# First projection block: the high part of x runs ahead of its low part, and the filter network's second layer moves four steps later

## The reference, cut to what matters

```python
xn = _rmsnorm(x, attn_norm_w)
proj = xn @ w_in                      # 1952 columns: hyena streams, q and kv latents, rotary key

h = jnp.sin(freq * (z @ filt_w1 + filt_b1))
h = jnp.sin(freq * (h @ filt_w2 + filt_b2))
h = h @ filt_w3                       # the implicit filters, multiplied by a decay table
```

## Time and profile before

| | |
|---|---|
| median of three runs | 1778.93 us (1777.25 to 1779.46) |
| the profiled execution, its own time | 1777.29 us |
| its span, first to last instruction | 1775.5 us |
| TensorE matmuls busy | 1730.4 us, 97% of the span, 10563 matmuls |
| DVE / ACT / POOL busy | 75% / 41% / 23% |
| mean granted TensorE clock | 0.996 |

### The profile page before, as it was taken

One profiled execution on the slowest core, in us unless ns is written; L12 is line 12 of the kernel. 1 busy time (PEld: TensorE's weight loads), 2 busy tenths in 40 slices (PEclk: granted clock), 3 DMA queues, 4 the chain that ended last, 5 costly groups with the idle time before them and its releaser, 6 DMA issues.

```text
span 1775.5 us, 26444 instructions
## 1 busy us (share of the span) xinstructions
PE 1730.4 (97%) x10563; PEld 1581.4 (89%) x10563; DVE 1338.2 (75%) x1677; ACT 728.8 (41%) x1149; POOL 407.8 (23%) x256
## 2 busy tenths in 40 slices
PE   7999999999999999998999999999899999999999
PEld 5776888887999988887999999999899999998887
DVE  6894676978998986779655555558999898996634
ACT  6122321166787785245333333334333333334411
POOL 0000000002222220003121222115758373740000
PEclk9999999999999999999999999999999999999999
DMA  9323154151100023433323223229141404002121
GB/s 358 130 71 131 70 200 149 51 183 57 43 22 22 16 84 98 144 122 125 126 92 107 88 97 102 88 90 356 60 154 59 156 31 156 29 1 78 37 95 60
DMA packets 59058, 183.65 MB, mean 103 GB/s; under 512 B 6901, under 2 KB 7669, under 8 KB 58424
## 3 DMA queue, kind: packets, MB, share of 16 engines
q1 hardware_dynamic: 58936, 181.96, 29.0%
HBM read 138.58 MB, written 43.35 MB: 102 GB/s over the span
## 4 chain that ended last, share of the span: by engine, by line
PE 83%; DVE 8%; DMA 3%; ACT 3%; issue 2%; SPq 1%; ACTq 0%; DVEq 0%
PE ps L3266 41%; PE ps L2742 23%; PE ps L3126 3%; PE ps L3154 3%; PE ps L3138 2%; PE ps L2802 2%; PE ps L2829 2%; PE ps L2841 2%; DVE ptl L2317 1%; DVE gmax L2270 1%; PE ps L3035 1%; DMA K<-decay 1%; PE ps L3047 1%; DMA wst<-wb 1%; DMA wst<-wm 1%
## 5 line engine op out<-in xcount | busy, mean ns | idle before, releaser
L3266 PE MATMUL ps<-rV,ringh 128*128 128x320 f32 x1248 | 235.8, 311 | 9.8 <-issue 7.8
L3266 PEld LDWEIGHTS ps<-rV,ringh 128*128 128x128 f32 x1248 | 197.2, 189 | 11.5 <-issue 9.0
L3266 PE MATMUL ps<-rU,ringh 128*128 128x320 f32 x1088 | 204.2, 309 | 2.6 <-issue 1.2
L2742 PE MATMUL ps<-XL,wh 128*128 128x512 f32 x708 | 177.6, 359 | 0.0
L2498 DVE TENSOR_TENSOR fH<-ps,fH 128x640 f32<-128x640 f32 x112 | 90.7, 821 | 110.5 <-PE ps L3266 110.4
L3266 PEld LDWEIGHTS ps<-rU,ringh 128*128 128x128 f32 x1088 | 170.5, 188 | 3.6 <-issue 2.3
L2742 PE MATMUL ps<-XH,wh 128*128 128x512 f32 (+1 forms) x612 | 162.4, 374 | 7.4 <-DVE wl L1637 3.4
L2742 PE MATMUL ps<-XH,wl 128*128 128x512 f32 (+1 forms) x612 | 153.3, 359 | 0.0
L3266 PE MATMUL ps<-rV,ringl 128*128 128x320 f32 x624 | 142.9, 310 | 0.0
L3266 PE MATMUL ps<-rH,ringh 128*128 128x320 f32 x736 | 137.9, 309 | 1.3 <-DVE rH L2443 1.3
L2742 PEld LDWEIGHTS ps<-XL,wh 128*128 128x128 f32 x708 | 118.2, 190 | 21.1
(11 more groups left out here) (414 smaller groups left out, 3895.4 us busy)
## 6 DMA issues: line engine op xcount, KB each, us to landing
hd<-fH SPq DMA_DIRECT2D x64, 320.0 KB, 2.3
wst<-wb SPq DMA_DIRECT2D x34, 512.0 KB, 3.7
wst<-wm SPq DMA_DIRECT2D x30, 512.0 KB, 3.9
fU<-hd SPq DMA_DIRECT2D x32, 320.0 KB, 4.0
fH<-hd SPq DMA_DIRECT2D x24, 320.0 KB, 4.0
wraw<-wm SPq DMA_DIRECT2D x14, 512.0 KB, 3.8
w2b<-wm SPq DMA_DIRECT2D x12, 512.0 KB, 7.3
xraw<-xT SPq DMA_DIRECT2D x8, 640.0 KB, 10.5
```

Of the source, the lines that this page charges most:

```text
L2742: ins = mm(acc(jslot)[:, o:o + n], sub(a[slot], s), b[:, o:o + n], start=(first and k == 0 and a is wh and b is xh), stop=(last and k == l ...
L3266: ins = mm(out[:, c, :], a[:, w], two(b(xs[kk]))[:, c, :], start=kk == 0 and a is h and b is hi_of, stop=kk == 3 and a is l)
```

## The change

Block 0 is no longer made by `block`. A new function `first_block` gives TensorE, for each k, the two passes that need only the high part of x (`wh` by `XH`, `wl` by `XH`), and the pass over the low part of tile k - 1 behind them. The second filter layer stands after the low pass of tile 5 (it stood after tile 2). ACT makes five high parts ahead of `filter_turns(0)` (it made two), `filter_sine(0)` and `split(B_IN + 1)` come later, all eight high parts stand ahead of that split, and `filter_turns(1)` stands directly behind it; all `token_sums` now come after `filter_turns(1)` (the first came ahead of it). DVE makes five low parts ahead of `argument(0)` (it made two), and `wl` of block 1 after all eight. The number of instructions of each kind is the same, and SP's list is untouched.

```diff
@@ ACT
-            x_hi_part(0)
-            x_hi_part(1)
+            for k in range(5):
+                x_hi_part(k)
             filter_turns(0)
-            for k in range(2, 5):
-                x_hi_part(k)
+            x_hi_part(5)
             filter_sine(0)
-            x_hi_part(5)
+            x_hi_part(6)
+            x_hi_part(7)
             split(B_IN + 1)
-            x_hi_part(6)
-            token_sums(0)
             filter_turns(1)
-            x_hi_part(7)
-            for t in range(1, 5):
+            for t in range(5):
                 token_sums(t)
             filter_sine(1)
             for t in range(5, 10):
@@ DVE
             split(B_IN, 0)
-            x_low(0)
-            x_low(1)
+            for k in range(5):
+                x_low(k)
             argument(0)
-            for k in range(2, 6):
+            for k in range(5, 8):
                 x_low(k)
             split(B_IN + 1, 1)
-            x_low(6)
-            x_low(7)
             argument(1)
@@ TensorE
+            def first_block():
+                def high(k):
+                    pe.wait_ge(x_hi, k + 1)
+                    for a in (wh, wl):
+                        for o, n in TOKENS:
+                            mm(acc(J_IN)[:, o:o + n], sub(a[0], k), tok(XH, k)[:, o:o + n], start=k == 0 and a is wh,
+                               stop=False)
+                def low(k):
+                    pe.wait_ge(x_lo, k + 1)
+                    for o, n in TOKENS:
+                        ins = mm(acc(J_IN)[:, o:o + n], sub(wh[0], k), tok(XL, k)[:, o:o + n], start=False,
+                                 stop=k == KD - 1)
+                    return ins
+                weights_ready(B_IN)
+                high(0)
+                for k in range(1, KD):
+                    high(k)
+                    low(k - 1)
+                    if k == 6:
+                        filter_layer(1)
+                low(KD - 1).then_inc(mm_done, 1)
...
-            def second_layer(k):
-                if k == 2:
-                    filter_layer(1)
...
             filter_layer(0)
-            block(0, second_layer, [(x_lo, k + 1) for k in range(KD)])
+            first_block()
             block(1, x_norm)
```

## The result

The changed kernel's median is 1781.43 us (14 runs) against 1778.49 (14 runs of the kernel before, beside it); the ratio is 1.0018, 95% interval 1.0011 to 1.0025. By that interval it is 2.0 to 4.4 us slower. The ratio itself is under the 0.2% (3.6 us) set as the bound of "no change"; the upper end of the interval is past it. The medians lie 2.94 apart. Forecast: +2.7, or 1781.6. The profiled execution took 1780.32 us, its span is 1778.6 against 1775.5.

A forecast was written before the change was run, and what follows sets the result against it. Row sums on ACT and the decay transfer, ending together near 53 us, bound the start; block 2 4.4 late, less 1.2 and 0.5 returned, gave +2.7 on 1778.93: 1781.6 us, own range 1780 to 1784, overall 1778.0 to 1784.5.

The forecast's parts named there:

- TensorE in block 0: Block 0 on TensorE: starts at 11.15 rather than 12.82, second filter layer at 25.6, ends at 30.0, 2.0 us ahead.
- ACT after it: ACT behind block 0's second filter layer: turns(1) not before 28.1, row sums ending at 41.07, +1.9 us by ACT alone.
- The transfers: SP's loads behind the first row sum: decay table +1.8 us (0.75 to 2.7), row sums +2.3.
- The wait and the clock: TensorE in block 1: 4.9 us wait for xdiag, then 1.2 GHz for 3.4 to 4.9 us, costing +2.1.
- The sum: From block 2 to the end: starts 4.4 us late, vanished waits return 1.2, further slack 0.5, leaving +2.7.
- Gain arrives: Rival at block 0: row sums no later, earlier start keeps its full 1.65 us, 1777.3; chance 0.15.
- Clock stays up: Rival at the xdiag wait: 4.9 us idle without a clock fall, decay decides, +1.8, 1780.7; chance 0.12.
- Absorbed: Rival behind 110 us: a wait with another cause takes up the delay, +0, 1778.9; chance 0.08.
- slower rival: Clock stays low through the wait ahead of block 2, slowing block 2 too: +4.4, 1783.3; chance 0.20.

The follow-up runs named there:

- pe_only: The kernel before with only TensorE's new block-0 pass order, second filter layer where it was, ACT's and DVE's lists as before; ratio 1.0002.
- best_after: Changed kernel, two row sums ahead of filter_turns(1), block 2's weight load ahead of five xt loads, its wl earlier on DVE, x_spread one k step later; ratio 0.9992.
- before_fill: The kernel before with block 2's weight load issued ahead of the last five xt loads and its wl made earlier on DVE; ratio 0.9991.
- layer_late: The kernel before with only the second filter layer moved, after tile 5 rather than tile 2 of block 0; ratio 1.0007.
- sums_first: The changed kernel with two row sums moved ahead of filter_turns(1) on ACT; ratio 1.0003.
- all_three: The changed kernel with two row sums ahead of filter_turns(1), 10 extra matmuls in the xdiag wait and decay's first quarter ahead of five xt loads; ratio 1.0007.
- keep_busy: The changed kernel with 20 extra matmuls, results overwritten, where TensorE waits for xdiag; ratio 1.0017.
- decay_early: The changed kernel with the decay table's first quarter issued ahead of the last five xt loads; ratio 1.0026.
- four: Changed kernel, two row sums ahead of filter_turns(1), 10 extra matmuls, decay's first quarter early, block 2's wl earlier on DVE; ratio 0.9998.

## Why the prediction was right

- **TensorE in block 0.** First matmul 10.87 (forecast 11.15; this execution's first tile landed 0.37 sooner), second layer 25.30 (25.6), block 1 at 29.78 (30.0). Right, and without value, as said. The Trainium skill, page "Perfetto Trace Analysis", section "Identifying the Most-Contended Engine", would have one optimize the busiest engine first; TensorE is that, and the 2 us won on it came back as idle (4.83). For this stretch the rule alone points to the wrong place, and pe_only (mark +0.07) and best_after (the same mark as before_fill) show it.
- **ACT after it.** Read of the layer 27.65 (28.1), `msx` 41.34 (41 to 42): +2.17 against +2.3. layer_late and sums_first show the cause from both sides: moving the layer alone makes `msx` 2.51 late, moving two row sums ahead of its read brings `msx` back to 39.31.
- **The transfers.** Decay +2.15 against +1.8 (bounds 0.75 and 2.7). The queue was thinner than the middle: 246 GB/s from 30 to 36. The size of the loads didn't set the rate: in best_after the queue moved 405 GB/s in the same stretch, its `xt` loads being the same 512 KB.
- **The wait and the clock.** 4.83 idle (4.9), and the clock fell as forecast. The slow stretch was mis-sized: `wl` was ready at 54.65, 3.78 late; less the sums' 2.17 that is 1.6 for the clock, where I took 2.1. The fall was likely rather than certain: after 2.14 us of idle in all_three the clock stayed at 1.00. The Trainium skill, page "TensorE: Matmul & The Clock Gate", section "What's actually happening", has slow as the default that activity lifts; the trace agrees (1.2 GHz after 4.83 us without matmuls, 1.00 again from 49 us on, with matmuls running since 45.33).
- **The sum.** Block 2 starts 3.78 late (forecast 4.4; the clock accounts for 0.5 of the difference and the sums for 0.1). The waits for decay and DVE give back 1.20, as forecast: the third `kernel_tile` of block 2 starts at 59.19, 2.58 late. Up to the mark only 0.23 more comes back, where I took 0.5. Together +2.35 at the mark against +2.7. The end came out at +3.1 in the profile because behind the mark it is 0.75 longer, which the sum doesn't have. That the total is so near is therefore partly luck, and so is the nearness of the medians: 1781.43 against 1781.6 comes from a step of 2.94 on a base of 1778.49, where I had 2.7 on 1778.93. As to the 0.75, one place is 330 to 336, where the granted clock was 1.00 before and 0.72 after. Which part of that belongs to the change and which to the single execution isn't settled: from the mark to the end the runs here take between 1694.4 and 1697.3 whatever their front, so spans of single executions aren't compared here.
- **Rivals.** "Gain arrives" fell with the 4.83. "Clock stays up" fell in the profile. keep_busy, where the clock does stay up, shows that decay then decides, as I wrote; its mark was +3.0, not my +1.8, 0.8 of that because decay landed later still. (Elsewhere the prediction prices an untouched clock at 0.8; this rival stands 0.9 below the forecast.) "Absorbed" fell: nothing behind the mark takes the delay back, the stretch from there to the end being 0.75 longer. Of the slower rival, the low clock until 51 didn't happen here but did in decay_early (+3.5 at the mark, 1.0026); there too it ended ahead of block 2, so its second step, a slow block 2, was seen nowhere.

## What to carry to other kernels

Before starting the busiest engine sooner, find what the stretch ends on; here it was a row sum on ACT and a transfer behind it in SP's list, and both hung on a read that the change put behind a later matmul group. Where two chains end together, an experiment on one can show nothing at the end; take both away, and measure each inside its own stretch. A load that waits for a consumer can leave the queue empty (33 GB/s here), and a load whose own wait is long over, moved ahead of it, fills the hole if it is small: 512 KB made the rate 386, while a 1280 KB piece in all_three and four made the loads behind it late.

## What the runs showed of the hardware

The granted clock fell to 0.50 around or after idle of 4.83 us (the changed kernel), 2.59 (layer_late), 2.56 (sums_first), 2.07 (four) and 2.04 (pe_only), and stayed at 1.00 after 2.14 (all_three), 1.25 (best_after) and 1.10 (before_fill). In these runs idle near 2 us went either way. In the changed kernel the clock was back by 48.6, some 3.3 us after the wait; in decay_early, after a wait of 5.07, not before 51. The first cost 1.6 us between `xdiag` and `wl`, the second 2.8. A repair that leaves 2.5 us of idle (sums_first) still pays that 1.6; with the sums early, moving one k step of work ahead of the wait (best_after, 1.25) avoided it with no extra work. From 30 to 36 us, with 512 KB loads issued one at a time as their buffers came free, the queue moved 213 (keep_busy), 246 (the changed kernel) and 300 GB/s (before); with one more such load queued ahead, 386 (before_fill).
